# The passage into the experts: the normalised stream rounded in natural order, then copied into the experts' order

## The chip, the cores and the metric

The kernel runs on one core of one Trainium2 chip. The metric is the device time of one execution in microseconds; the time of a kernel is the median of its runs.

## The reference

One layer of a hybrid encoder on 16 meta tokens and 256 tokens of width 2048, in float32. A token mixer (latent attention and retention) is followed by a layer norm and a mixture of experts:

```python
h = layer_norm(ALPHA * h + mix, ln1_g[l], ln1_b[l])
...
g_sel = jnp.argmax(g_logits + b_group.astype(jnp.float32), axis=-1)
...
_, e_local = lax.top_k(e_logits + e_bias, TOP_K)
...
return (jax.nn.silu(xb @ w1[e]) * (xb @ w3[e])) @ w2[e]
...
h = layer_norm(ALPHA * h + ffn, ln2_g[l], ln2_b[l])
return h[:, N_META:]
```

Each token goes to one of 4 groups of experts and to 2 of the 8 experts of that group. There are 32 experts; each has w1 and w3 of 2048 x 512 and w2 of 512 x 2048.

## The kernel before

The kernel multiplies float32 matrices as sums of products of rounded parts. A value is rounded to the type F32R (the high part), and the difference of the value and its high part is the low part. In most places ScalarE makes the high part and VectorE the low part; TensorE multiplies with both.

The kernel goes through the mixer's stages and then through the passage that is changed here. After the last product of the mixer (w_out), VectorE has the sum of the residual and the mixer's output in `mrg`, two tiles (t = 0, 1) of 128 tokens by 2048. It normalises them in place: first with the mean and the gain (L766), then with the standard deviation and the offset (`stream`, L773), which raises `s_h1` once for each tile. From there:

- ScalarE rounds a tile from `mrg` into `xh1` (L738) and raises `s_xh1`. `mrg` holds column d = 16 p + k at place d. `xh1` and `xl1` hold it in the experts' order, k outside and p inside, because the experts' weights are laid on the partitions with 16 neighbouring rows each. So L738 reads with a step of 16 elements (64 bytes) and writes one element after another.
- VectorE does the routing in some 30 small operations, ends them with the selection matrix `pg` (`gather_matrix`, L843, `s_pg`), and then subtracts `xh1` from `mrg` into `xl1` (`stream_rest`, L779, `s_xl1`), again reading `mrg` with the step.
- TensorE computes the logits, keeps itself busy with matmuls that nobody reads (`keep_warm`, L1059) while VectorE routes, and then gathers the first pair's tokens: it waits for `pg` and for both tiles of `xh1`, runs `first_gather` for the high part (L1099), three keep-warms, the low part of the first tile, eight keep-warms, the low part of the second:

```python
keep_warm(4, 0)
pe.wait_ge(s_pg, 1)
pe.wait_ge(s_xh1, TT)
for q in range(7):
    first_gather(q, 0, (0, 1))
for t in range(TT):
    keep_warm(8 if t else 3, 0)
    pe.wait_ge(s_xl1, t + 1)
```

- ScalarE copies the gathered columns from PSUM into `xg` (`gathered`, L641), TensorE multiplies them with the first expert's weights.

The experts' stage works on units of 1 MB of weights. Numbered from 0, 24 of them make a pair of experts. SyncE's queue loads a unit into a ring (`load`, L504); ScalarE rounds it (`hi`, L636), VectorE subtracts (`lo`, L786), TensorE multiplies (L1119 with the high part, L1120 with the low). Two units of 24, and unit 0, go to TensorE unrounded (L1116). The order of each engine's work is written out by hand. Of the first units some are loaded early: 0 to 3 during the mixer; 4, 5 and 8 to 11 after the last unit of w_out is used; 6 and 7 when `xl1` of the first and of the second tile is done, because they lie where `mrg` was. Units 12 to 15 wait until TensorE is done with units 0 to 3, and unit n from 16 on until it is done with unit n - 8. At the stage's end the stream comes back from `xh1` and `xl1` into the sum (L1215), for the second tile through `evens` (L707), which ScalarE writes with a step of 16 elements from contiguous input.

Of the kernel before, what the change touches and what calls it, by code (L numbers as in the profile page):

```python
# [5 lines left out]
F32 = mybir.dt.float32  # L6
F32R = mybir.dt.float32r
I32 = mybir.dt.int32
U32 = mybir.dt.uint32
ALU = mybir.AluOpType  # L10
ACT = mybir.ActivationFunctionType
AXX = mybir.AxisListType.X

P = 128
D_MODEL = 2048
KD = D_MODEL // P
N_META = 16
SEQ = 256
TT = SEQ // P
# [72 lines left out]
def moe_trunk(nc, ins, out):  # L92
# [5 lines left out]
    def place(name, shape, at, dtype=F32):  # L98
        size = 4
        for s in shape[1:]:  # L100
            size *= s
        assert base + at + size <= end, (name, base + at + size, end)
        return nc.alloc_sbuf_tensor_at(name, shape, dtype, offset=base + at)

    def sem(name):
        return ctx.enter_context(nc.semaphore(name))

    with ctx:
# [10 lines left out]
        mrg = place("mrg", [P, TT, D_MODEL], 165888)  # L119
# [180 lines left out]
        wl_e = {n: place(f"wl_e{n}", [P, U], at, F32R) for n, at in EARLY_AT.items()}  # L300
        xh1 = place("xh1", [P, TT, KD, P], 98304, F32R)
        xl1 = place("xl1", [P, TT, KD, P], 114688, F32R)
        xg = place("xg", [P, 2, KD, 2, 2 * SLOTS], 131072, F32R)
        yt = place("yt", [P, KD, SEQ], 115712)
        hx = place("hx", [P, KF, 2 * SLOTS], 163840, F32R)
# [63 lines left out]
        s_co = sem("s_co")  # L369
        s_yt = sem("s_yt")  # L370
        s_ytc = sem("s_ytc")
        s_xh1 = sem("s_xh1")
        s_xl1 = sem("s_xl1")
        s_lgt = sem("s_lgt")
# [251 lines left out]
        def scalar_experts(act):  # L626
# [108 lines left out]
            hi(0, 1)  # L735
            for t in range(TT):
                act.wait_ge(s_h1, t + 1)
                nc.scalar.activation(xh1[:, t, :, :], mrg[:, t, :].rearrange("q (p k) -> q k p", k=KD),  # L738
                                     ACT.Copy).then_inc(s_xh1, 1)
            for x in (2, 3, 4):  # L740
                hi(0, x)
# [14 lines left out]
        def vector_experts(dve, own):  # L756
# [18 lines left out]

            def stream_rest(t):

                dve.wait_ge(s_xh1, t + 1)
                nc.vector.tensor_tensor(xl1[:, t, :, :], mrg[:, t, :].rearrange("q (p k) -> q k p", k=KD),  # L779
                                        xh1[:, t, :, :].bitcast(F32), ALU.subtract).then_inc(s_xl1, 1)  # L780

            def lo(turn, x):
                if whole(turn, x):
# [64 lines left out]
            for t in range(TT):  # L848
                stream_rest(t)
# [493 lines left out]
        def _(act):  # L1343
# [191 lines left out]
            act.wait_ge(s_lgt, 1)  # L1535
            nc.scalar.activation(lgt[:, :], ps[0:N_GROUPS + N_EXP, 0, 0:SEQ], ACT.Copy).then_inc(s_lgc, 1)
            scalar_experts(act)


# [891 lines left out]
```

## Time and profile before

| | |
|---|---|
| time, median of 3 runs | 2134.16 us (2133.64 to 2135.18) |
| span of the profiled execution | 2134.4 us, 0.2 us over the median |
| TensorE matmuls busy | 2069.4 us (97%) |
| VectorE busy | 1592.3 us (75%) |
| ScalarE busy | 1286.2 us (60%) |
| loads of weights and all else by the hardware queue | 598.01 MB |

The profile is of one execution. Its span runs from the first to the last instruction. The busy shares are means over stages that differ: the experts' stage begins at about 1126 us and takes nearly half of the span. Times in rows are microseconds from the span's start unless marked ns. Ends of matmuls are modelled.

### The profile page before, as it was taken

How to read it: one execution, taken by the hardware profiler on the slowest of the kernel's cores; microseconds unless marked ns; L12 is line 12 of the kernel's file. 1: busy time of each engine (PE TensorE's matmuls, PEld its weight loads, DVE VectorE, ACT ScalarE, POOL GpSimd, SP SyncE). 2: the span in 40 equal slices, each digit the busy share in tenths (PEclk: the TensorE clock that was granted, in tenths of full speed). 3: DMA queues.
4: the chain of work that ended last, by engine and by line, in shares of the span. 5: the costliest groups of instructions: out<-in, count | busy, mean ns of one | idle time of the engine just before them, and what ended most of it. 6: DMA issues, size and time to landing. Idle time of an engine off the chain costs nothing.

```text
span 2134.4 us, 30028 instructions
## 1 busy us (share of the span) xinstructions
PE 2069.4 (97%) x11452; PEld 1749.8 (82%) x11452; DVE 1592.3 (75%) x1450; ACT 1286.2 (60%) x1064; POOL 104.7 (5%) x76
## 2 busy tenths in 40 slices
PE   8999999999999999999999999999999999999986
PEld 8998888899999998887887777777777787777764
DVE  7646664453646375455669999999999999999988
ACT  5445653333333323334347888888888888888883
POOL 1000000000000000001000000000000000000010
PEclk9999999999999999999999999999999999999998
DMA  6554335655454544557777999999999999999996
GB/s 215 159 139 158 118 120 186 208 180 172 146 176 148 166 157 143 192 197 239 233 297 287 399 421 421 421 420 419 418 420 418 421 418 417 417 417 418 417 397 251
DMA packets 168608, 606.48 MB, mean 284 GB/s; under 512 B 20252, under 2 KB 32684, under 8 KB 117452
## 3 DMA queue, kind: packets, MB, share of 16 engines
q1 hardware_dynamic: 164976, 598.01, 73.9%
q0 software_dynamic: 3552, 7.37, 1.1%
q8 instruction: 55, 0.90, 0.2%
q14 instruction: 25, 0.20, 0.0%
HBM read 595.05 MB, written 22.04 MB: 289 GB/s over the span
## 4 chain that ended last, share of the span: by engine, by line
PE 64%; DVE 16%; issue 9%; DMA 7%; ACT 3%; DVEq 0%; POOLq 0%; POOL 0%; SPq 0%; ACTq 0%
PE ps L1991 19%; PE ps L1972 15%; DVE wl L786 11%; DMA raw<-in_w_dram 7%; PE ps L1119 5%; PE ps L1120 5%; PE ps L2349 4%; PE ps L1116 3%; ACT wh L636 2%; PE ps L2104 2%; PE ps L1141 1%; DVE yall L951 1%; PE ps L2064 1%; PE ps L1089 1%; PE ps L2077 1%
## 5 line engine op out<-in xcount | busy, mean ns | idle before, releaser
L786 DVE TENSOR_TENSOR wl<-raw,wh 128x2048 fp32r<-128x2048 f32 x347 | 780.9, 2288 | 39.7 <-ACT wh L636 38.4
L636 ACT ACTIVATE wh<-raw 128x2048 fp32r<-128x2048 f32 x347 | 661.6, 1915 | 132.8 <-DMA raw<-in_w_dram 72.6
L1548 DVE TENSOR_TENSOR wl<-raw,wh 128x2048 fp32r<-128x2048 f32 (+1 forms) x168 | 379.8, 2263 | 283.3 <-ACT wh L1350 283.3
L1350 ACT ACTIVATE wh<-raw 128x2048 fp32r<-128x2048 f32 (+1 forms) x168 | 317.9, 1895 | 444.6 <-DMA raw<-in_w_in_dram 264.7
L1119 PE MATMUL ps<-wh,xg 128*128 128x512 f32 x896 | 373.1, 416 | 25.0 <-DVE wl L786 24.5
L1120 PE MATMUL ps<-wl,xg 128*128 128x512 f32 x880 | 345.2, 392 | 0.0
L1972 PE MATMUL ps<-hth,wh 128*128 128x272 f32 (+1 forms) x896 | 259.8, 290 | 3.1 <-DVE wl L1548 1.8
L1972 PE MATMUL ps<-htl,wh 128*128 128x272 f32 (+1 forms) x896 | 255.7, 285 | 0.0
L1972 PE MATMUL ps<-hth,wl 128*128 128x272 f32 (+1 forms) x896 | 255.6, 285 | 0.0
L1119 PEld LDWEIGHTS ps<-wh,xg 128*128 128x128 f32 x896 | 169.1, 189 | 77.2 <-DVE wl L786 28.3
L1119 PE MATMUL ps<-wh,hx 128*128 128x512 f32 x508 | 202.4, 398 | 3.5 <-DVE wl L786 1.9
L1120 PE MATMUL ps<-wl,hx 128*128 128x512 f32 x508 | 198.6, 391 | 0.0
L1120 PEld LDWEIGHTS ps<-wl,xg 128*128 128x128 f32 x880 | 166.3, 189 | 37.8 <-issue 7.2
L1972 PEld LDWEIGHTS ps<-hth,wh 128*128 128x128 f32 x896 | 168.9, 188 | 5.8 <-DVE wl L1548 2.4
L1972 PEld LDWEIGHTS ps<-htl,wh 128*128 128x128 f32 x896 | 168.8, 188 | 0.3
L1972 PEld LDWEIGHTS ps<-hth,wl 128*128 128x128 f32 x896 | 168.6, 188 | 0.0
L1991 PE MATMUL ps<-wh,hth 128*128 128x512 f32 x384 | 156.1, 406 | 0.0
L1991 PE MATMUL ps<-wh,htl 128*128 128x512 f32 x384 | 151.3, 394 | 0.0
L1991 PE MATMUL ps<-wl,hth 128*128 128x512 f32 x384 | 150.8, 393 | 0.0
L1116 PE MATMUL ps<-raw,xg 128*128 128x512 f32 x256 | 115.1, 592 | 1.0 <-ACT xg L641 1.0
L1119 PEld LDWEIGHTS ps<-wh,hx 128*128 128x128 f32 x508 | 95.6, 188 | 24.1 <-issue 3.3
L597 POOL DMA_INDIRECT yscr<-yall,dest x30 | 67.6, 2255 | 887.5 <-DVE yall L951 887.5
(379 smaller groups left out, 3116.7 us busy)
## 6 DMA issues: line engine op xcount, KB each, us to landing
raw<-in_w_dram SPq DMA_DIRECT2D x380, 1024.0 KB, 10.4
raw<-in_w_in_dram SPq DMA_DIRECT2D x103, 1024.0 KB, 5.1
raw<-in_w_pa_dram SPq DMA_DIRECT2D x16, 1024.0 KB, 5.0
raw<-in_w_pb_dram SPq DMA_DIRECT2D x16, 1024.0 KB, 5.0
raw<-in_w_out_dram SPq DMA_DIRECT2D x16, 1024.0 KB, 5.1
raw<-in_w_ukv_dram SPq DMA_DIRECT2D x8, 1024.0 KB, 5.3
raw_e<-in_w_dram SPq DMA_DIRECT2D x4, 1024.0 KB, 8.1
yscr<-zeros SPq DMA_DIRECT2D x4, 1024.0 KB, 10.7
```

The costliest lines, as they stand in the source:

```text
L597: pool.indirect_dma_start(yscr[:, :], bass.IndirectOffsetOnAxis(dest[0:SLOTS, par:par + 1], 0), yall[own_rows(par), :], None, bounds_check ...
L636: nc.scalar.activation(wh2[:, x % HELD, :], raw_of(turn, x), ACT.Copy).then_inc(s_wh2, 1)
L786: nc.vector.tensor_tensor(wl_of(turn, x), raw_of(turn, x), wh2[:, x % HELD, :].bitcast(F32), ALU.subtract).then_inc(s_wl2, 1)
L1116: m = nc.tensor.matmul(o, s.bitcast(F32), raw_of(turn, x)[:, c:c + 512], start=st, stop=sp_, skip_group_check=True)
L1119: nc.tensor.matmul(o, s, wh2[:, x % HELD, c:c + 512], start=st, stop=False, skip_group_check=True)
L1120: m = nc.tensor.matmul(o, s, wl_of(turn, x)[:, c:c + 512], start=False, stop=sp_, skip_group_check=True)
L1350: nc.scalar.activation(wh[:, n % RING1, 0:c], raw1[:, n % RING1, 0:c], ACT.Copy).then_inc(s_wh, 1)
L1548: nc.vector.tensor_tensor(wl[:, n % RING1, 0:c], raw1[:, n % RING1, 0:c], wh[:, n % RING1, 0:c].bitcast(F32), ALU.subtract).then_inc(s_wl, 1)
L1972: m = nc.tensor.matmul(ps[:, bank, col:col + width], w[:, n % RING1, c:c + P], s[:, 4 * u + k, c0:c0 + width], start=opens and u == 0 and ...
L1991: m = nc.tensor.matmul(ps[:, bank + t, :], s[:, 4 * u + k, c:c + P], w[:, n % RING1, 512 * k:512 * (k + 1)], start=u == 0 and k == 0 and j ...
L2104: m = nc.tensor.matmul(ps[:, bank + b, col:col + SEQ], w[:, n % RING1, c:c + P], s[:, k, X0:LT], start=opens and k == 0 and j == 0, stop=k ...
L2349: m = nc.tensor.matmul(ps[:, bank + t, :], s[:, 4 * u + k, P * t:P * (t + 1)], w[:, n % RING1, 512 * k:512 * (k + 1)], start=u == 0 and k ...
```

## The change

The rounding from `mrg` is done in natural order into a new tile `xnh` (both tiles of tokens), and a second ScalarE instruction for each tile copies from `xnh` to `xh1`, reading one element after another and writing with a step of 128 elements. VectorE's subtraction waits for `s_xnh` instead of `s_xh1`, reads `mrg` and `xnh` in natural order and writes `xl1` with that step. `xnh` lies where the first half of `xg` is written afterwards. TensorE's waits are unchanged.

```diff
+        xnh = place("xnh", [P, TT, D_MODEL], 131072, F32R)
...
+        s_xnh = sem("s_xnh")
...
             hi(0, 1)
             for t in range(TT):
                 act.wait_ge(s_h1, t + 1)
-                nc.scalar.activation(xh1[:, t, :, :], mrg[:, t, :].rearrange("q (p k) -> q k p", k=KD),
+                nc.scalar.activation(xnh[:, t, :], mrg[:, t, :], ACT.Copy).then_inc(s_xnh, 1)
+            for t in range(TT):
+                act.wait_ge(s_xnh, t + 1)
+                nc.scalar.activation(xh1[:, t, :, :].rearrange("q k p -> q p k"),
+                                     xnh[:, t, :].bitcast(F32).rearrange("q (p k) -> q p k", k=KD),
                                      ACT.Copy).then_inc(s_xh1, 1)
             for x in (2, 3, 4):
                 hi(0, x)
...
             def stream_rest(t):

-                dve.wait_ge(s_xh1, t + 1)
-                nc.vector.tensor_tensor(xl1[:, t, :, :], mrg[:, t, :].rearrange("q (p k) -> q k p", k=KD),
-                                        xh1[:, t, :, :].bitcast(F32), ALU.subtract).then_inc(s_xl1, 1)
+                dve.wait_ge(s_xnh, t + 1)
+                nc.vector.tensor_tensor(xl1[:, t, :, :].rearrange("q k p -> q p k"),
+                                        mrg[:, t, :].rearrange("q (p k) -> q p k", k=KD),
+                                        xnh[:, t, :].bitcast(F32).rearrange("q (p k) -> q p k", k=KD),
+                                        ALU.subtract).then_inc(s_xl1, 1)
```

## Rows read from the trace of the kernel before

**Rows 1.** Windows by stage: start:end, length, busy us of each engine, granted clock, DMA share, GB/s.

```profile
1145.00:1150.00 5.00, 5.00 (x32) 4.41 (x31) 4.93 (x7) 4.31 (x7) 0.00 (x0) 1.00 0.00 0
1150.00:1155.00 5.00, 5.00 (x19) 3.24 (x18) 4.35 (x22) 4.75 (x4) 0.00 (x0) 1.00 0.61 210
1300.00:1500.00 200.00, 195.35 (x972) 155.88 (x972) 190.85 (x131) 169.84 (x125) 15.76 (x7) 1.00 1.01 420
```

**Rows 2.** Timeline of SyncE's queue: start, length, instruction, count.

```profile
1130.06 26.47 SPq L504 DMA_DIRECT2D raw<-in_w_dram  x7
```

**Rows 3.** The chain of waits, passage and first weights: start, length, engine and line.

```profile
1117.42 3.34 PE ps L1099 x28
1120.76 0.72 PE ps L1059 x6
1121.48 1.51 PE ps L1099 x14
1122.99 1.84 PE ps L1059 x16
1124.83 0.34 PE ps L1099 x2
...
1156.27 1.91 ACT wh L636
```

**Rows 4.** Timeline of VectorE in the passage.

```profile
1105.04 4.62 DVE L773 SCALAR_TENSOR_TENSOR mrg<-mrg,rstd,ln1b 128x2048 f32<-128x2048 f32 x2
...
1116.94 0.43 DVE L843 TENSOR_TENSOR pg<-slots,rk__167 128x256 fp32r<-128x256 f32 x1
1117.28 7.38 DVE L779 TENSOR_TENSOR xl<-mrg,xh 128x2048 fp32r<-128x2048 f32 x2
...
1124.97 6.69 DVE L786 TENSOR_TENSOR wl<-raw,wh 128x2048 fp32r<-128x2048 f32 x3
```

**Rows 5.** Timeline of ScalarE in the passage.

```profile
1109.38 7.36 ACT L738 ACTIVATE xh<-mrg 128x2048 fp32r<-128x2048 f32 x2
1116.62 3.72 ACT L636 ACTIVATE wh<-raw 128x2048 fp32r<-128x2048 f32 x2
1120.23 1.92 ACT L636 ACTIVATE wh<-raw_e 128x2048 fp32r<-128x2048 f32 x1
1125.19 1.08 ACT L641 ACTIVATE xg<-ps 128x512 fp32r<-128x512 f32 x2 [3.05 <-PE ps L1099]
```

**Rows 6.** Timeline of TensorE: the last keep-warms ahead of the first gather.

```profile
1116.20 1.14 PE L1059 MATMUL ps<-ident,ones 128*128 128x128 f32 x8
```

**Rows 7.** Line 707: duration in ns (min, median, max), start, form.

```profile
L707 ACT ACTIVATE even_lo<-xl x1: 3852/3852/3852, 2040.1 to 2040.1; 128x2048 fp32r<-128x2048 f32 x1
L707 ACT ACTIVATE even_hi<-xh x1: 3792/3792/3792, 2061.4 to 2061.4; 128x2048 fp32r<-128x2048 f32 x1
```

**Rows 8.** Timeline of TensorE at the stage's end: stepped operands, then contiguous ones.

```profile
2104.68 0.75 PE L1215 MATMUL ps<-xl,identr 128*128 128x512 f32 x1
2105.24 0.72 PE L1215 MATMUL ps<-xh,identr 128*128 128x512 f32 x1
...
2112.35 0.40 PE L1215 MATMUL ps<-even_hi,identr 128*128 128x512 f32 x1
2112.59 0.40 PE L1215 MATMUL ps<-even_lo,identr 128*128 128x512 f32 x1
```

**Rows 9.** Timeline of TensorE around two idle gaps (in brackets), and the same transposes without one.

```profile
1002.14 5.38 PE L2315 MATMUL ps<-ident,mrg 128*128 128x128 f32 x32 [2.68 <-DVE mrg L1746]
1096.59 3.65 PE L2326 MATMUL ps<-ident,mrg 128*128 128x128 f32 x32
2064.52 0.77 PE L1119 MATMUL ps<-wh,xg 128*128 128x512 f32 x1 [2.68 <-DVE wl L786]
2067.21 0.58 PE L1119 MATMUL ps<-wh,xg 128*128 128x512 f32 x1
```

**Rows 10.** A window of 1 us after the first of these gaps (columns as in rows 1).

```profile
1003.00:1004.00 1.00, 1.00 (x7) 1.00 (x6) 0.96 (x3) 0.95 (x4) 1.00 (x2) 0.50 1.06 410
```

## The prediction, made before the result was known

> **What bounds the kernel now.** I read the windows by stage first. In the experts' stage the DMA engines are the limit: from 1300 to 1500 us their share is 1.01 and they move 420 GB/s, while VectorE is at 191 of 200 us. Just after the routing they stand still: share 0.00 from 1145 to 1150 us [rows 1]. The reader should see that this hole lies between two stages in which the queue is full, so it is lost for good, and its length is set by whoever lets the queue go on.
>
> Who that is comes out of the code and the DMA queue's own timeline. From unit 12 on, SyncE loads a unit only when TensorE has finished an older one: units 12 to 15 wait for units 0 to 3, unit 16 for unit 8. The burst of these loads begins at 1130.06, when unit 0 ends [rows 2]. So what TensorE reaches later, the weights reach later.
>
> Then the chain of waits through the passage: from 1117.42 to 1125.17 it is TensorE alone: 28 gathers of the rounded stream, three keep-warm matmuls, 14 gathers of the difference, eight keep-warms, 2 gathers [rows 3]; then two ScalarE copies, 1.08 us together from 1125.19 [rows 5], and unit 0. The keep-warms stand in TensorE's order and run whatever the others do.
>
> What lets this row begin? It needs three things. VectorE's selection matrix (pg) ends at 0.43 after 1116.94, that is 1117.37 [rows 4]. The two stepped roundings on ScalarE (L738) run from 1109.38 for 7.36 us, to 1116.74 [rows 5]. The keep-warms ahead end at 1116.20 + 1.14 = 1117.34 (the ends are modelled) [rows 6]. VectorE is last; ScalarE has 0.6 us of slack and no more. The differences on VectorE take 7.38 from 1117.28 [rows 4], and TensorE comes to each as it is ready.
>
> **The change, part by part.** *Removed:* ScalarE's two stepped reads. *Added:* two natural roundings into xnh, and two copies from it with a step of 512 bytes on the write side (128 four-byte elements between neighbours). These are four instructions in ScalarE's queue where two were, and nothing that TensorE's first gathers wait for (s_xh1) is shortened: it now follows all four.
>
> Natural roundings: two of the same shape (L636) start 3.61 apart from the next, 1116.62 to 1120.23, so 1.8 us each [rows 5]. The first can start where L738 starts; the second tile of the stream is there at 1105.04 + 4.62 = 1109.66 [rows 4], before it is wanted. The copies begin at 1109.38 + 3.61 = 1112.99.
>
> Stepped copies: no row has a 512-byte step on the write side. Below, a copy could cost no more than a contiguous one, 1.8 to 1.9 us [rows 5]. The nearest row is ScalarE writing the same number of elements with a 64-byte step from contiguous input: 3.79 and 3.85 us [rows 7]. Above, TensorE reading xh1 with just this 512-byte step starts its matmuls 0.56 apart (2104.68, 2105.24), and with contiguous operands 0.24 apart (2112.35, 2112.59) [rows 8]; that ratio of 2.3 on 1.9 us gives 4.4 us. I take 3.82: same engine, same side, same count. Two back to back overlap by 0.1, as the two of L738 do (twice 3.73 in 7.36), so 7.54: xh1 is whole at 1120.53 instead of 1116.74.
>
> By the Trainium skill, "Vector Engine (DVE) Microarchitecture Reference", section 5.2, a port that hops on every element is slow on either side: about 1.73 ns a column with one source hopping and 1.71 with the destination alone. The trace agrees for the read: 7.38 us for two differences of 2048 columns with one stepped source [rows 4]. For a write of this step no run here shows it; an estimate by 1.71 is 3.5 us a copy and the end 0.6 us below the sum. The page speaks against the change: moving the step to the other side would save nothing.
>
> TensorE: it starts 0.05 after its release (1117.37 to 1117.42), so at 1120.58: **3.16 us** later.
>
> Then the clock. TensorE's last keep-warms end at 1117.34, so it stands idle for some 3.2 us where it now waits 0.1. Two idle gaps of 2.68 us in this trace, before 1002.14 and before 2064.52, are each followed by matmuls at half their pace; the granted clock after the first is 0.50, 1.2 GHz instead of 2.4 [rows 9, 10]. A gap longer than both makes the fall the likelier case. Its price: the 32 transposes after the first gap took 5.38 us, the same 32 at full clock 3.65 [rows 9], so 1.73 at most. A part of the slow time can fall into the idle gap itself; after the second gap the first and the seventh matmul start 2.69 apart (2064.52, 2067.21), which six steps of 0.24 would make 1.44, so 1.25 lost at least [rows 8, 9]. I take **1.5 us**.
>
> *The difference's other order:* VectorE now waits for s_xnh, ready by 1113.1, which is earlier; it is still busy with routing until 1117.28, so nothing is gained there. Its two instructions go from a stepped source to a stepped destination. Below: 2.3 us each, the price of a contiguous subtraction (6.69 for three) [rows 4]; above: 2.3 times that, 5.2; I take the present 3.7. None of the three moves the end. If cheap, the last difference is ready at 1121.9 while TensorE, late by itself, asks for the first only after its 28 gathers and three keep-warms, near 1124.6. If 5.2, the first is ready at 1122.5 and the second near 1127.7, where TensorE asks at about 1128.0 without a slow clock and later with one. Behind them on VectorE stand four weight subtractions; with the present price they go on from 1124.97 as now, and unit 1's, the first of them, is done by 1127.3, while TensorE must first do unit 0, which now ends at 1130.06 [rows 2]. SyncE's loads of units 6 and 7 wait for s_xl1 and move with VectorE alone: nothing or at most 3 us, and ScalarE wants them only after its eight gather copies and unit 5. The change issues no DMA.
>
> *Queued behind ScalarE's longer row:* three weight roundings (units 2 to 4). They start 3.8 later and end at about 1126 instead of 1122.15 [rows 5]. That is still before TensorE's first two gather banks are full, near 1128.3, and ScalarE now idles there until 1125.19 [rows 5]. So they cost nothing; without the cover, what exceeds 1128.3 would come on top.
>
> *Does the delay reach the end?* From unit 0 on, the chain of waits is TensorE, with the copies of its own gathers; the first other step in it is a weight rounding at 1156.27 [rows 3], when unit 8 is done and the loads go on [rows 1]. So units 0 to 3 and 8 are late by the same amount, the hole in the DMA grows by it, and behind it a queue at 1.01 can catch up nothing. I count all of it.
>
> Sum: 3.16 + 1.5 = 4.66 us. The profiled execution's span is 2134.4, the median of the runs 2134.16, 0.2 less; against the median the sum is 2138.8 us, 0.22% more. A measurement of this kernel can tell about 0.2%, which is 4.3 us.
>
> **The rivals.**
> *The clock stays.* If the 3.2 us do not lower it, only the wait remains: 2134.16 + 3.16 = 2137.3, within 0.2%. For it: one can't tell from two gaps that every such gap brings a fall. Against: both shorter ones did.
>
> *The write side is cheap* (not slower). If ScalarE's 512-byte write runs like a contiguous one, the place is the wait for s_xh1 ahead of the first gather, and the price 2 x 1.8 from 1112.99, so 1116.6, under pg's 1117.37. TensorE then starts as now: 2134.2. It decides as soon as a copy takes less than about 2.2 us. It gains nothing either, since TensorE's row is fixed from pg on. Against it: the 64-byte write at 3.8 [rows 7].
>
> *The step is dearer.* At 4.4 us a copy xh1 is whole at 1112.99 + 8.7 = 1121.7, TensorE waits 4.3 longer, and with the fall the end is 2134.16 + 5.8 = 2140.0. For it: TensorE pays more for this step than a factor of two [rows 8]. Against: ScalarE's own stepped write stays at two [rows 7]. The page of the Trainium skill named above gives 2.50 ns for a destination that steps 24 words; an estimate by it is 5.1 us a copy and an end near 2141.5, and no row here is so dear.
>
> *Absorbed behind.* If VectorE or the DMA queue had slack between 1150 and 1200 us, part would come back; half of it gives 2136.5. For it: the DMA share is 0.61 from 1150 to 1155 [rows 1], so the queue is not yet the limit. Against: what limits it there is TensorE, which is late itself.
>
> **How the numbers follow.** Forecast with the fall 0.50; clock stays 0.20; dearer step 0.12; absorbed 0.10; cheap write 0.08. The likeliest gives 2138.8; its own spread, with 1.2 to 1.73 for the clock and 3.7 to 3.9 for a copy, is 2138.2 to 2139.1. The range from 2136.2 to 2140.6 holds the forecast, the case without the fall, most of the dearer and about half of the absorbed; it leaves out the cheap write and the tails. Slower by over 0.2%: four fifths of the forecast, which lies close to that bound, and the dearer step, 0.51; within: the rest of the forecast and the other cases, 0.45; faster, with no path that I can find: 0.04.
>
> **What would show it.** In the changed profile: two ScalarE copies of about 1.9 and two of about 3.8 us from 1109.4 on; an idle gap of TensorE of some 3.2 us ahead of its first gather, put down to ScalarE; a granted clock of 0.50 somewhere in 1118 to 1125 us; the differences still near 3.7 us; unit 0 ending, and the burst of loads beginning, 3 to 5 us later; the hole in the DMA as much longer. The prediction is wrong if the copies take less than 2.2 us or well over 4, or if the experts' stage ends no later although TensorE's gathers do.

## The result, and the profile after

The changed kernel takes 2143.59 us (median of five, 2141.86 to 2145.55), the kernel before 2134.16 beside it: a ratio of 1.0044, with an interval from 1.0032 to 1.0056. It is slower by 9.4 us, twice what was forecast (4.7). Its profiled execution took 2143.56 us with a span of 2141.7; the difference, 1.9 us, lies around the span.

ScalarE's timeline in the passage (start, length, line, tiles, count) answers to [rows 5]:

```profile
1110.30 3.70 ACT L740 ACTIVATE xnh<-mrg 128x2048 fp32r<-128x2048 f32 x2
1113.90 7.29 ACT L743 ACTIVATE xh<-xnh 128x2048 fp32r<-128x2048 f32 x2
1121.01 3.70 ACT L638 ACTIVATE wh<-raw 128x2048 fp32r<-128x2048 f32 x2
1124.61 1.89 ACT L638 ACTIVATE wh<-raw_e 128x2048 fp32r<-128x2048 f32 x1
1133.82 1.08 ACT L643 ACTIVATE xg<-ps 128x512 fp32r<-128x512 f32 x2 [7.31 <-PE ps L1107]
```

Everything starts 0.92 us later than before (1110.30 for 1109.38); that comes from the mixer, which the change doesn't touch, and is taken off below. From there the new row goes as foreseen: 3.60 us from the first rounding to the first copy, 7.29 us for the two copies, and `xh1` whole at 1121.19. The three weight roundings end at 1126.50, and ScalarE then stands idle for 7.31 us.

TensorE's timeline answers to [rows 3] and [rows 6] (idle time and releaser in brackets):

```profile
1117.11 1.14 PE L1067 MATMUL ps<-ident,ones 128*128 128x128 f32 x8
1121.34 5.09 PE L1107 MATMUL ps<-pg,xh 128*128 128x128 f32 x28 [3.10 <-ACT xh L743]
1126.23 1.59 PE L1067 MATMUL ps<-ident,ones 128*128 128x128 f32 x6
1127.47 3.23 PE L1107 MATMUL ps<-pg,xl 128*128 128x128 f32 x14
1130.50 3.11 PE L1067 MATMUL ps<-ident,ones 128*128 128x128 f32 x16
1133.37 0.64 PE L1107 MATMUL ps<-pg,xl 128*128 128x128 f32 x4
1134.96 3.70 PE L1124 MATMUL ps<-raw,xg 128*128 128x512 f32 x8 [0.95 <-ACT xg L643]
```

The gap is there, 3.10 us, put down to ScalarE's copies. What follows it is not 1.5 us longer than before but far more: every group up to the eight keep-warms takes longer (a keep-warm is two matmuls in these rows). From the first gather to the copies of the first bank pair it is 1133.82 - 1121.34 = 12.48 us, where it was 1125.19 - 1117.42 = 7.77 [rows 3, 5]. That is 4.7 us on top of the gap. The windows say why (start:end length, busy of TensorE, its weight loads, VectorE, ScalarE, GpSimd; granted clock, DMA share, GB/s):

```profile
1120.00:1125.00 5.00, 3.66 (x23) 3.69 (x23) 5.00 (x2) 5.00 (x4) 0.00 (x0) 0.76 1.07 364
1125.00:1130.00 5.00, 5.00 (x25) 5.00 (x25) 4.97 (x5) 1.51 (x1) 0.00 (x0) 0.50 1.01 359
1130.00:1135.00 5.00, 4.05 (x25) 3.91 (x24) 4.66 (x3) 1.08 (x2) 0.00 (x0) 0.72 0.27 115
1135.00:1140.00 5.00, 4.72 (x18) 2.67 (x18) 0.00 (x0) 1.13 (x3) 0.00 (x0) 1.00 0.05 10
1145.00:1150.00 5.00, 5.00 (x28) 4.20 (x27) 4.57 (x3) 5.00 (x5) 0.00 (x0) 1.00 0.99 380
1155.00:1160.00 5.00, 5.00 (x27) 4.25 (x27) 4.76 (x11) 4.30 (x8) 0.00 (x0) 1.00 0.00 0
1300.00:1500.00 200.00, 196.06 (x984) 157.38 (x983) 191.30 (x125) 170.59 (x127) 15.75 (x7) 1.00 1.01 421
```

A window at 0.76 that holds only the two levels 1.0 and 0.5 was at half clock for 0.48 of its 5 us, so 2.4; one at 0.72 for 2.8. With the 5 us between them TensorE ran at 1.2 GHz for 10.2 us, that is to the end of the eight keep-warms. The DMA queue has emptied by 1135 (share 0.05), works again, and stands still a second time from 1155 to 1160; before, it was still for one stretch [rows 1]. In the experts' stage it is as full as ever.

VectorE's two differences are unchanged (against 7.38 in [rows 4]), and SyncE's burst answers to [rows 2]:

```profile
1118.18 7.37 DVE L785 TENSOR_TENSOR xl<-mrg,xnh 128x2048 fp32r<-128x2048 f32 x2
```

```profile
1138.69 34.31 SPq L506 DMA_DIRECT2D raw<-in_w_dram  x9
```

The burst begins 8.63 later than before: 0.92 from the mixer, 3.0 from the wait (1121.34 - 0.92 - 1117.42) and 4.7 from the clock. The chain of waits carries the whole of it on (start, length, what):

```profile
1117.47 3.74 ACT xh L743
...
1164.90 1.91 ACT wh L638
```

The copy has come into the chain, and the weight rounding that stood at 1156.27 [rows 3] now stands at 1164.90, again 8.63 later. At the end of the span 7.3 us of it are left (2141.7 for 2134.4).

### The profile page after: what moved, and what is told of

It reads as the page before. It is cut to its first block, busy times and chain, and to the rows that moved or that the text cites. A ratio compares the mean times of both kernels' runs of the same rounds, so it can differ in the third digit from the quotient of the medians.

```text
span 2141.7 us, 30030 instructions
## 1 busy us (share of the span) xinstructions
PE 2074.2 (97%) x11452; PEld 1753.5 (82%) x11452; DVE 1590.6 (74%) x1450; ACT 1288.0 (60%) x1066; POOL 104.8 (5%) x76
## 3 DMA queue, kind: packets, MB, share of 16 engines
q0 software_dynamic: 3552, 7.37, 1.1%
## 4 chain that ended last, share of the span: by engine, by line
PE 64%; DVE 16%; issue 9%; DMA 7%; ACT 3%; DVEq 0%; POOLq 0%; POOL 0%; SPq 0%; ACTq 0%
PE ps L1999 19%; PE ps L1980 15%; DVE wl L794 11%; DMA raw<-in_w_dram 6%; PE ps L1127 5%; PE ps L1128 5%; PE ps L2357 4%; PE ps L1124 3%; ACT wh L638 2%; PE ps L2112 2%; PE ps L1149 1%; DVE yall L959 1%; PE ps L2072 1%; PE ps L2085 1%; PE ps L1097 1%
## 6 DMA issues: line engine op xcount, KB each, us to landing
raw<-in_w_dram SPq DMA_DIRECT2D x380, 1024.0 KB, 10.2
```

## The experiments

My theory was that the price is the wait plus a long stay at half clock. The rivals: the stepped write itself, by contention or by what it does to the gathers' operand; or something behind the passage. Medians are compared with the runs of the kernel before that were made beside them.

**e1_warm: fill the gap.**

```diff
             pe.wait_ge(s_pg, 1)
+            keep_warm(13, 0)
             pe.wait_ge(s_xh1, TT)
```

> The changed kernel with 13 more keep-warm matmuls on TensorE (0.23 us each, 3.0 us) between its wait for the selection matrix and its wait for xh1; nothing else differs. Theory: of the loss some 3.1 us are the wait for xh1, and the rest is TensorE at half clock (0.50 from 1122.57 to 1132.81 us in the profile) after it stood idle. Then here no granted clock below 1.00 in the passage, the 28 gathers back at about 3.3 us, unit 0 some 3.2 us later than in the kernel before, time 2137.3 us. Rival: the gathers are slow because VectorE's stepped writes into SBUF run beside them, whatever the clock. Then the gathers still take about 5 us and the passage about 12, time about 2142.

Measured: 2138.14 us (2136.48 to 2139.36, eleven runs) beside 2135.56, ratio 1.0009 (1.0000 to 1.0018). TensorE's timeline and a window over the rest of the passage:

```profile
1114.43 4.38 PE L1067 MATMUL ps<-ident,ones 128*128 128x128 f32 x34
1118.66 3.34 PE L1107 MATMUL ps<-pg,xh 128*128 128x128 f32 x28
```

```profile
1122.00:1126.00 4.00, 4.00 (x39) 4.00 (x37) 3.97 (x5) 1.92 (x2) 0.00 (x0) 1.00 1.04 349
```

The data arrive as late as before the filling: this execution's selection matrix began at 1115.16, 1.78 before that of [rows 4], so its first gather is 3.0 us late for this execution. But the gathers take 3.34 us, as in [rows 3], at full clock, from the same stepped copies. So the stepped write is not what slows the gathers, and of the 9.4 us between the medians 2.6 stay with the wait; the other 6.8 go when the gap is filled.

**e2_cold: a slow clock without any stepped write.** The kernel before, without the keep-warm in the routing's loop.

```diff
                 pe.wait_ge(s_dve, step_)
-                keep_warm(1)
```

> The kernel before without the keep-warm matmuls between the routing's steps (those of the loop over the routed steps; the 12 ahead of it stay), so that TensorE stands idle for some 4 us ahead of the routing's last matmuls; ScalarE's and VectorE's work is as in the kernel before, so the gathers should start within 0.5 us of 1117.4. Theory (half clock lasts through the passage): gathers 5 us, passage from the first gather to unit 0's release about 12 instead of 7.8 us, time 2138 to 2139. Prediction as it was put (the fall costs at most 1.73 us): 2135.9. Rival (stepped writes slow the gathers): there are none here, so 2134.2.

Measured: 2142.18 us (2140.18 to 2144.15, nine runs), ratio 1.0028 (1.0018 to 1.0038): 6.6 us slower. TensorE's timeline and a window:

```profile
1115.52 0.61 PE L1074 MATMUL ps<-asg,before 128*128 128x32 f32 x2 [4.58 <-DVE asg L830]
...
1118.50 6.21 PE L1098 MATMUL ps<-pg,xh 128*128 128x128 f32 x28
...
1125.76 3.23 PE L1098 MATMUL ps<-pg,xl 128*128 128x128 f32 x14
1128.78 3.65 PE L1059 MATMUL ps<-ident,ones 128*128 128x128 f32 x16
```

```profile
1126.00:1130.00 4.00, 4.00 (x21) 4.00 (x21) 4.00 (x3) 0.00 (x0) 0.00 (x0) 0.50 0.99 359
```

The gap is 4.58 us here. The first gather is only 1.08 late, yet the passage to the first copies takes 14.1 us (1118.50 to 1132.64) for 7.77 [rows 3, 5]: 28 gathers in 6.21 us, and half clock for 17.1 us, from 1115.2, still in the gap, to about the end of the eight keep-warms. I had expected a passage of 12 us and 2138 to 2139, so my theory had the price too low as well. The gathers at half clock are dear whatever wrote their operand.

**e3_direct: the step on the write side alone.** The kernel before, with ScalarE reading `mrg` in order and writing `xh1` with the step, in two instructions.

```diff
-                nc.scalar.activation(xh1[:, t, :, :], mrg[:, t, :].rearrange("q (p k) -> q k p", k=KD),
+                nc.scalar.activation(xh1[:, t, :, :].rearrange("q k p -> q p k"),
+                                     mrg[:, t, :].rearrange("q (p k) -> q p k", k=KD),
```

> The kernel before with the write-side step alone: ScalarE rounds straight from mrg into xh1, reading in natural order and writing with the 512-byte step, two instructions as before; no xnh, VectorE as before. Theory: the side of the step does not matter (3.75 us each either way), what costs is that there are four instructions; xh1 is whole where it was, time 2134.2, clock 1.00 in the passage. Rival: the written step disturbs others or is dearer by itself; then xh1 late, or gathers slower, 2136 or more.

Measured: 2134.70 us (2132.99 to 2138.53, twelve runs), ratio 0.9995 (0.9987 to 1.0004). The line's durations in ns (min, median, max):

```profile
L738 ACT ACTIVATE xh<-mrg x2: 3775/3784/3793, 1109.0 to 1112.6; 128x2048 fp32r<-128x2048 f32 x2
```

The write costs 3.78 us where the read cost 3.73. The side of the step doesn't matter to the time, as expected. What the changed kernel has besides, the two roundings put ahead of the copies, is what makes `xh1` late.

**e4_first and e7_first_warm: half the wait.** In both, the weight rounding that stands ahead of the stream on ScalarE is done behind it; e7_first_warm also fills what gap is left.

```diff
-            hi(0, 1)
...
-            for x in (2, 3, 4):
+            for x in (1, 2, 3, 4):
...
             pe.wait_ge(s_pg, 1)
+            keep_warm(6, 0)    (e7_first_warm alone)
```

> The changed kernel with the rounding of weight unit 1 (1.9 us on ScalarE) moved from ahead of the stream's roundings to behind them. ScalarE then begins the stream when its first tile is there and is through with xh1 some 1.5 us after the selection matrix instead of 3.1. Theory: the wait shrinks to 1.5 us, TensorE's idle gap too, and the clock stays at 1.00; so more than half of the loss goes with 1.6 us of wait: time 2135.7. If the cost were the wait alone: 9.4 less 1.6, about 2142. Rival (stepped writes slow the gathers): about 2140.

> The fourth experiment (changed kernel, rounding of unit 1 behind the stream's) with six more keep-warms ahead of the wait for xh1, so that the 1.6 us gap is filled. Its median was 2141.2, spread from 2135.2 to 2147.7, with mean granted clocks from 0.996 to 0.990. Theory: the spread and all of the loss beyond 1.6 us is the clock, which falls after this short gap in most executions and not in others; filled, the clocks are all 0.995 or 0.996 and the time 2136 to 2137, with a spread of 3 us. Rival: the reordering itself costs (VectorE's subtraction of unit 1, or ScalarE's later roundings): 2140 still.

Measured: e4_first 2141.21 us (2135.24 to 2147.71, twelve runs), ratio 1.0024 (1.0012 to 1.0035); e7_first_warm 2135.83 (2134.56 to 2140.58, twelve runs) beside 2134.55, ratio 1.0004 (0.9995 to 1.0012). The profiled execution of e4_first:

```profile
1119.05 3.31 PE L1106 MATMUL ps<-pg,xh 128*128 128x128 f32 x28 [1.67 <-ACT xh L742]
```

That execution took 2138.31 us and kept its clock through a gap of 1.67 us. Most of the others, it seems, didn't: in nine of twelve the mean granted clock was 0.994 or less, and the two quickest, 2135.24 and 2135.62, had 0.996. I had expected 2135.7 and no fall after so short a gap, and the time was wrong. By its median alone e4_first would fit the other reading, that the whole price is the wait (2142). But filling the gap brings 4.4 us back (5.65 above the kernel before beside it, then 1.28) with the wait as it was, so most of the loss is the clock. Where the slow time lay in the unprofiled executions is inferred from that, not seen.

**e8_again: the changed kernel once more,** for the spread of the slow stretch; no edit.

> The changed kernel as it is, beside the others on the same chip. Theory: 2143 to 2144 with mean clocks of 0.991 to 0.993 in every execution, since its gap of 3.1 us is longer than any that left the clock alone. If the fall were a matter of chance at 3.1 us too, some executions would lie near 2137.

Measured: 2144.21 us (2141.67 to 2145.53, six runs), ratio 1.0039 (1.0027 to 1.0051). TensorE's timeline, and windows:

```profile
1119.78 5.60 PE L1107 MATMUL ps<-pg,xh 128*128 128x128 f32 x28 [3.11 <-ACT xh L743]
...
1129.44 3.72 PE L1067 MATMUL ps<-ident,ones 128*128 128x128 f32 x16
```

```profile
1120.00:1125.00 5.00, 5.00 (x28) 5.00 (x27) 4.97 (x5) 4.95 (x3) 0.00 (x0) 0.54 1.07 333
1125.00:1130.00 5.00, 5.00 (x25) 5.00 (x25) 5.00 (x3) 0.00 (x0) 0.00 (x0) 0.50 0.91 364
1130.00:1135.00 5.00, 4.25 (x20) 4.02 (x20) 3.10 (x2) 1.09 (x2) 0.00 (x0) 0.59 0.04 18
```

The same gap, and half clock for 4.6 + 5 + 4.1 = 13.7 us. The gathers and keep-warms up to the first copies (1133.52) take 13.74 us, 6.0 more than before. This passage begins 0.67 earlier than that of [rows 6] (its last keep-warms at 1115.53), and its burst of loads at 1138.39: 8.33 after the 1130.06 of [rows 2], so 9.0 late. The span, 2142.7, is 8.3 longer than before's, with the 0.67 again 9.0. In this execution nothing came back behind the passage, and in the first one 1.3 us did. So the loss doesn't arise behind the passage, and the third explanation is out as well.

**e9_dense and e10_narrow: work behind the gap, ahead of the gathers.** Both leave the gap as it is. Nobody reads the extra matmuls.

```diff
             pe.wait_ge(s_xh1, TT)
+            for _ in range(6):    (e9_dense)
+                nc.tensor.matmul(ps[:, 0, :], ones[:, :], xh1[:, 0, 0:4, :].bitcast(F32), ...)
+            keep_warm(23, 0)    (e10_narrow, in its place)
```

> The changed kernel with six float32 matmuls of 512 columns (0.86 us each at full clock, 5.2 in all; nothing reads them) right behind the wait for xh1, ahead of the gathers. With the next kernel it asks whether what runs behind the gap sets how long the clock stays at half. Theory: it does; here the clock is back within 3.4 to 7 us and the gathers behind run at full clock, so that this kernel loses 3.1 of wait, 5.2 of added work and 1.7 to 3.4 of slow clock: 2144 to 2146, though it does more than the changed kernel. Rival: the length has nothing to do with what runs; then this kernel and the next come out alike, both near 2149.

> The same with 23 keep-warm matmuls of 128 columns (0.23 us each at full clock, 5.2 in all) in that place. Theory: they keep the clock low as the gathers do, so that added work and passage run at half clock for 10 us or more: 2148 to 2151, mean clocks of 0.990 to 0.992, and a spell in the profile longer than that of the kernel with wide matmuls. Rival: as the kernel with wide matmuls, within 1 us.

Measured: e9_dense 2144.73 us (2143.21 to 2148.78, five runs) beside 2135.44, ratio 1.0046 (1.0032 to 1.0059); e10_narrow 2145.08 (2144.41 to 2148.63, five runs), ratio 1.0048 (1.0034 to 1.0062). TensorE in e9_dense, with its windows:

```profile
1120.56 5.39 PE L1262 MATMUL ps<-xh,ones 128*128 128x512 f32 x12 [3.10 <-ACT xh L743]
1125.39 3.64 PE L1107 MATMUL ps<-pg,xh 128*128 128x128 f32 x28
```

```profile
1122.00:1126.00 4.00, 4.00 (x13) 1.85 (x11) 3.97 (x4) 3.73 (x3) 0.00 (x0) 1.00 1.05 328
1126.00:1130.00 4.00, 4.00 (x39) 4.00 (x37) 4.00 (x3) 0.00 (x0) 0.00 (x0) 1.00 0.98 410
```

And in e10_narrow, with its windows:

```profile
1120.30 7.00 PE L1067 MATMUL ps<-ident,ones 128*128 128x128 f32 x46 [3.08 <-ACT xh L743]
1127.06 3.32 PE L1107 MATMUL ps<-pg,xh 128*128 128x128 f32 x28
```

```profile
1122.00:1126.00 4.00, 4.00 (x26) 4.00 (x26) 3.97 (x4) 3.47 (x2) 0.00 (x0) 0.67 1.04 334
1126.00:1130.00 4.00, 4.00 (x39) 4.00 (x37) 4.00 (x3) 0.00 (x0) 0.00 (x0) 1.00 0.96 356
```

I had expected the wide matmuls to bring the clock back and the narrow keep-warms not to. In the profiled e10_narrow it came back while the keep-warms ran; in the profiled e9_dense it never fell in the passage. In both the gathers then ran at full clock, unlike in the two profiled executions of the changed kernel, with the same gap of 3.1 us. The unprofiled executions point the same way: the mean granted clock was 0.994 or more in eight of these ten, and 0.992 or 0.993 in all eleven of the changed kernel. So the added work shortens the slow stretch in most executions. Whether it is wide or narrow made no difference that these runs show, against my theory, and the rival's 2149 for both was wrong too. The whole is no quicker, since the extra work itself takes 4.8 us (1120.56 to 1125.39; I had reckoned 5.2) and 6.8 (1120.30 to 1127.06): behind the gap it costs as much as it saves, in the gap (e1_warm) it is free.

**e5_wide: wide matmuls among the gathers.** The changed kernel, with the three and eight keep-warms replaced by one and two matmuls of 512 columns.

```diff
-                keep_warm(8 if t else 3, 0)
+                for _ in range(2 if t else 1):
+                    nc.tensor.matmul(ps[:, 0, :], ones[:, :], xh1[:, 0, 0:4, :].bitcast(F32), ...)
```

> The changed kernel with the eleven keep-warm matmuls between the gathers (three and eight, 128 columns each) replaced by one and two float32 matmuls of 512 columns into the same bank; they too compute nothing that is read. Question: the slow clock lasted 3.4 us after the two gaps of the kernel before, where 128x128 transposes and 512-column matmuls followed, and 10.2 us here, where gathers of 128 columns with a weight load each and narrow keep-warms follow. Theory: what runs after the gap keeps the clock low; with wide matmuls in between it comes back sooner, the half-clock spell is 7 us or less, time 2140 to 2142. Rival: the spell is as long whatever runs (it comes from the gap or from the routing ahead of it): 10 us again, 2143.5 or more.

Measured: 2142.17 us (2141.14 to 2148.06, six runs), ratio 1.0030 (1.0018 to 1.0042). That is some 2 us better than the changed kernel at the most, with intervals that overlap, and the clock was still at half for 10.2 us of the profiled passage. That execution, the slowest of the six at 2148.06, had a second long slow stretch in the last stage, 13.7 us:

```profile
2070.00:2080.00 10.00, 8.28 (x30) 7.45 (x31) 8.36 (x4) 7.23 (x5) 3.87 (x2) 0.55 0.96 388
2080.00:2090.00 10.00, 10.00 (x28) 6.38 (x27) 4.42 (x8) 4.39 (x3) 0.00 (x0) 0.76 0.49 169
```

It settles nothing on what wide matmuls do in the passage.

**e6_split: no filler at all.** The kernel before, with the differences in four parts, so that TensorE always has a gather to do and unit 0 comes ahead of the later ones. The core of the edit:

```diff
-            for t in range(TT):
-                stream_rest(t)
+            for k0, k1 in ((0, 4), (4, KD)):
+                for t in range(TT):
+                    stream_rest(t, k0, k1)
...
-            for q in range(7):
+            for q in range(4):
+                first_gather(q, 0, (0, 1))
+            pe.wait_ge(s_xl1, TT)
+            for q in range(2):
+                first_gather(q, 1, (0, 1))
+            for q in range(4, 7):
                 first_gather(q, 0, (0, 1))
-            for t in range(TT):
-                keep_warm(8 if t else 3, 0)
-                pe.wait_ge(s_xl1, t + 1)
-                for q in range(2 if t else 7):
-                    first_gather(q, 1, (t,))
```

Five more low gathers follow unit 0, behind a wait for the last two parts.

> The kernel before (stepped reads, no xnh) with the differences in four parts, for the columns of the first two gathers (k 0 to 3) of both token tiles first, the rest behind; TensorE gathers both parts of the first two banks as soon as these are there and begins unit 0, the other differences' gathers follow unit 0; the eleven keep-warms between go; ScalarE copies the first two gathers before it rounds unit 4; the loads of units 6 and 7 wait for the third and fourth part. Theory: what TensorE reaches earlier in the passage comes out at the end like what it reaches later: unit 0 begins 3 us earlier (1123.3 instead of 1126.3), unit 1 about 3.5, later units 2.5 to 3, so time 2131.5 beside 2134.2. Rival (the experts' stage has slack of its own, the passage counts only where it stops the clock): 2134.2.

Measured: 2132.43 us (2130.53 to 2132.88, eleven runs) beside 2134.55, ratio 0.9986 (0.9978 to 0.9995): quicker than both kernels. TensorE's timeline and SyncE's burst:

```profile
1117.54 2.00 PE L1104 MATMUL ps<-pg,xh 128*128 128x128 f32 x16
1119.48 1.11 PE L1104 MATMUL ps<-pg,xl 128*128 128x128 f32 x8
1120.43 1.50 PE L1104 MATMUL ps<-pg,xh 128*128 128x128 f32 x12
1121.77 3.65 PE L1121 MATMUL ps<-raw,xg 128*128 128x512 f32 x8
```

```profile
1125.45 9.16 SPq L504 DMA_DIRECT2D raw<-in_w_dram  x4
```

The burst begins 4.6 us ahead of [rows 2]. At the end of the two spans 3.7 of it are left (2130.7 for 2134.4), but that execution of the kernel before was itself some 2 us above its median; between the medians it is 2.1, where 2.7 was expected. So an earlier passage does reach the end, against the rival; how much of it does, these runs don't settle.

## Why the prediction was half right

**The wait: right.** 3.16 us were forecast; the first gather is 3.0 late, the gap 3.10, and with the clock kept up (e1_warm) the kernel loses 2.6.

**The step on the write side: right.** 3.82 us a copy were forecast from the 64-byte write of [rows 7]; the 512-byte write took 3.73 and 3.77 in the changed kernel and 3.78 in e3_direct. The dearer step and the cheap write are both out. The sentence from the Trainium skill, "Vector Engine (DVE) Microarchitecture Reference", section 5.2, that the port pays for hopping on either side, is borne out for VectorE's difference: 7.37 us for 2 x 2048 columns, 1.8 ns a column where the page has 1.71 for a hop of 4 KiB.

**The difference's order and ScalarE's longer row: right.** Both are hidden: 7.37 for 7.38 us, and the last weight rounding ends at 1126.50, 7.31 us before ScalarE is wanted.

**The fall of the clock: right. Its price, 1.5 us with "1.73 at most": this is the step that failed.** It measured 4.7 us in one execution of the changed kernel and 6.0 in the other; between the medians it is 6.8 (9.4 less the 2.6 of e1_warm). The price was read off two gaps in one execution, followed by other work: 32 transposes, or the experts' matmuls of 512 columns [rows 9]. At these two places (the first taken as 1000 to 1014 us) the twelve profiled executions were at half clock for 3.4 us in eighteen cases of twenty-four, not at all in three, and for 6.8, 10.2 and 13.7 us in one each. In the passage, with the gathers behind the gap, TensorE stayed at half clock through nearly the whole of them: 10.2 and 13.7 us in the changed kernel, 10.2 in e5_wide, 17.1 in e2_cold. I had taken the length of the slow stretch as if it belonged to the gap, and two cases as its bound. It differs from place to place, and from one execution to the next at the same place; by e9_dense and e10_narrow against the changed kernel, work put behind the gap changes it too. Why, no run shows. I had also thought that part of it might lie within the idle time. It didn't: the clock fell about 1.2 us after the first gather had started (1122.6), and in e8_again 0.7 us after.

**The pass to the end: right in the main.** In e8_again it is whole (9.0 at the loads, 9.0 at the end); in the first profiled execution 8.6 at the loads became 7.3, so up to 1.3 us came back. The rival by which half would be absorbed is out.

**The sum.** With the measured clock it is 3.0 + 4.7 to 6.0, so 7.7 to 9.0 us; the medians differ by 9.4 and 9.7. The last 0.4 to 2 us are not put down to anything. There was one slip besides: I set the span of before, 2134.4, beside the median of the times, and called it 0.2 us over, though in the changed kernel 1.9 us lie around the span. With the same 1.9 the profiled execution of before was about 2 us above its median, which is why the two profiles differ by 7.3 and the medians by 9.4. In the chances, four fifths of the forecast and the dearer step are 0.52, not 0.51; nothing rests on that.

**What stays open.** What sets the length of the slow stretch: why the same gap was followed by 10.2 us of half clock in one execution, 13.7 in another, and none in the profiled e9_dense; and how short a gap is harmless, since 1.67 us ahead of the gathers kept its clock in the profiled execution and, by the mean clocks, cost it in most others.

## What to carry to other kernels

An engine that is "nearly last" at a meeting point (here ScalarE, with 0.6 us to spare) can't be given more work without counting the wait; and where TensorE is the one that waits, the wait can be the smaller part of the price. Price a fall of the clock by gaps that are followed by the same kind of work as yours, not by the gap's length, and take one or two such rows as cases, not as a bound. If no such row exists, reckon with half clock for the whole of the work behind the gap: here that would have been 7.8 us, the passage once more, where 4.7, 6.0 and, in e2_cold, 6.4 were measured. In this passage matmuls that nobody reads were free ahead of the wait and as dear as the fall behind it; quicker than either was an order in which TensorE had real work at that place (e6_split).

## What the hardware showed that I had not expected

Through gathers of 128 columns, one behind another and with TensorE busy all the time, the clock stayed down: 0.50 from 1125 to 1130 us with TensorE busy for 5.00 of 5 us. In a row of keep-warms directly behind the same gap it was back after 3.4 us at half clock (0.67 over 1122 to 1126, then 1.00; the fall began at 1121.2). The Trainium skill, "TensorE: Matmul & The Clock Gate", Part 1, says that the throttled state is the default and that activity releases it. That agrees with e10_narrow; the changed kernel adds that the clock stayed down all the while that TensorE was busy with these gathers. Nor is that particular to gathers. In the same execution of the changed kernel there was half clock for 6.8 us in the mixer, from about 1006.5 us on, while TensorE ran one matmul of 512 columns behind another; part of the 0.92 us by which everything starts later may come from there:

```profile
1008.00:1012.00 4.00, 4.00 (x10) 3.08 (x10) 4.00 (x2) 1.39 (x1) 2.18 (x3) 0.50 1.06 360
```

The slow stretch is also not tied to this passage: in the profiled execution of e7_first_warm, the slowest of its twelve, it lay in the last stage, behind the gap that [rows 9] shows at 2064.52:

```profile
2060.00:2070.00 10.00, 7.25 (x30) 5.67 (x29) 8.60 (x5) 9.99 (x8) 2.26 (x1) 0.85 1.01 418
2070.00:2080.00 10.00, 10.00 (x28) 6.76 (x28) 7.12 (x9) 2.95 (x3) 1.44 (x1) 0.64 0.65 247
```

That is half clock for 3.0 + 7.2 = 10.2 us, where the kernel before had it for 3.4 behind the same gap, in a part of the program that the edit doesn't touch:

```profile
2060.00:2070.00 10.00, 7.32 (x36) 5.96 (x36) 8.83 (x4) 9.26 (x7) 2.26 (x1) 0.83 1.01 409
2070.00:2080.00 10.00, 10.00 (x39) 6.97 (x39) 8.54 (x10) 6.72 (x7) 1.34 (x1) 1.00 0.91 336
```

One execution is thus a weak witness for the price of a fall.
